# Expert blocks of 32 places instead of 64, with two buffers for the rows that come in and two for the results that go out

## The reference

```python
def hier_moe(xn, w_group, b_group, w_expert, b_expert, w1, w3, w2):
    """Top-1 expert group, then top-2 SwiGLU experts inside that group."""
    ...                                   # eid: 2 of 32 experts for each token, ew: their weights
    def expert_block(args):
        xb, e = args
        return (jax.nn.silu(xb @ w1[e]) * (xb @ w3[e])) @ w2[e]
    ...                                   # out[t] = sum over its two experts of ew * y
```

## Time and profile before

| | us |
|---|---|
| time of three runs | 1649.1, 1653.12, 1655.06 (median 1653.12) |
| the profiled execution's own time | 1650.04 |
| its span | 1648.4 |
| granted clock of TensorE over the span | 0.988 |
| PE busy | 1564.9 (95%) |
| DMA over the span | 328.42 MB, mean 199 GB/s |
| expert stage, first to last of its matmuls | 1050.4 to 1603.2 |

### The profile page before, as it was taken

The page is one execution under the profiler, slowest core; times in us unless marked ns, Lnnn a source line. Parts: engine busy times, 40 slices in busy tenths (PEclk is TensorE's granted clock), DMA queues, the critical chain, the costliest instruction groups (busy, mean ns, idle before and its releaser), DMA issues.

```text
span 1648.4 us, 21863 instructions
## 1 busy us (share of the span) xinstructions
PE 1564.9 (95%) x7698; PEld 848.1 (51%) x7699; DVE 560.9 (34%) x1542; ACT 346.8 (21%) x859; POOL 300.6 (18%) x431
## 2 busy tenths in 40 slices
PE   7999998999999999998999999799899999999986
PEld 4554544444444444444444555566466666666652
DVE  4210004766566656654222354511011111111115
ACT  3000002443343443433000111111111111111113
POOL 2000001322222222222001001221121212121114
PEclk9999999999999999998999999999999999999997
DMA  9214621553111110103443821699999989999928
GB/s 236 67 56 62 125 78 58 166 181 114 45 32 26 45 33 26 46 13 90 161 136 103 357 107 74 235 416 419 419 419 418 386 352 407 416 421 417 415 85 306
DMA packets 135914, 328.42 MB, mean 199 GB/s; under 512 B 40046, under 2 KB 80398, under 8 KB 126640
## 3 DMA queue, kind: packets, MB, share of 16 engines
q1 hardware_dynamic: 117472, 297.98, 49.5%
q0 software_dynamic: 9984, 17.62, 3.2%
q10 hardware_dynamic: 8400, 12.07, 2.1%
HBM read 276.09 MB, written 55.25 MB: 201 GB/s over the span
## 4 chain that ended last, share of the span: by engine, by line
PE 83%; DVE 7%; DMA 5%; issue 2%; ACT 2%; POOL 1%; SPq 1%; POOLq 0%; ACTq 0%; DVEq 0%
PE PS L856 17%; PE PS L707 12%; PE PS L591 11%; PE PS L870 9%; PE PS L745 7%; PE PS L780 7%; PE PS L693 4%; PE PS L654 4%; PE PS L673 4%; PE PS L586 3%; DMA WA<-w 2%; PE PS L833 2%; DMA BA<-hn_d,ids 1%; POOL WA L1532 1%; PE PS L573 1%
## 5 line engine op out<-in xcount | busy, mean ns | idle before, releaser
L707 PE MATMUL PS<-WA 128*128 128x512 f32 x512 | 255.0, 611 | 2.2 <-ACT WA L967 1.6
L856 PE MATMUL PS<-WA,BA 128*64 128x256 f32 x2048 | 227.6, 379 | 2.9 <-DMA WA<-w 1.5
L856 PEld LDWEIGHTS PS<-WA,BA 128*64 128x64 f32 x2048 | 173.9, 137 | 63.9 <-issue 17.3
L591 PE MATMUL PS<-WA,BA 128*128 128x512 f32 x416 | 180.1, 593 | 2.9 <-DVE WA L1090 2.9
L1450 POOL TENSOR_SCALAR BA<-BA,rin,gates 128x640 f32<-128x640 f32 (+7 forms) x128 | 99.6, 781 | 270.8 <-DVE rin L1209 270.8
L1364 DVE SCALAR_TENSOR_TENSOR BA<-BA,PS 128x256 f32<-128x256 f32 x46 | 19.4, 422 | 340.8 <-ACT BA L1029 340.8
L591 PEld LDWEIGHTS PS<-WA,BA 128*128 128x128 f32 x416 | 78.6, 190 | 99.6 <-issue 96.2
L673 PEld LDWEIGHTS PS<-ident,BA 128*128 128x128 f32 x648 | 79.4, 144 | 94.1 <-issue 86.6
L870 PE MATMUL PS<-WA,BA 128*64 128x512 f32 x512 | 116.9, 597 | 9.7 <-DVE BA L1374 8.7
L707 PEld LDWEIGHTS PS<-WA 128*128 128x128 f32 x512 | 84.6, 190 | 78.4 <-issue 67.6
L957 ACT ACTIVATE BA<-PS,ngm 128x640 f32<-128x640 f32 (+7 forms) x128 | 89.9, 702 | 130.5 <-DVE ngm L1187 126.1
(11 more groups left out here) (249 smaller groups left out, 1548.4 us busy)
## 6 DMA issues: line engine op xcount, KB each, us to landing
WA<-w SPq DMA_DIRECT2D x66, 2048.0 KB, 25.3
BA<-w SPq DMA_DIRECT2D x30, 2048.0 KB, 27.6
rows_d<-WA SPq DMA_DIRECT2D x8, 2048.0 KB, 9.5
rows_d<-BA ACTq DMA_DIRECT2D x92, 128.0 KB, 6.8
WA<-w_in SPq DMA_DIRECT2D x16, 512.0 KB, 5.6
gates_d<-WA SPq DMA_DIRECT2D x32, 256.0 KB, 2.4
WA<-gates_d SPq DMA_DIRECT2D x8, 1024.0 KB, 5.4
BA<-w_in SPq DMA_DIRECT2D x26, 256.0 KB, 6.1
```

The costliest lines, as they stand in the source:

```text
L591: mm = pe.matmul(PS[:, j % 4, :], ws[:, c % 6, k, :], hnT[:, k, 512 * h:512 * h + 512], start=(k == 0), stop=(k == KT - 1))
L707: mm = pe.matmul(PS[:, 6, :], gw[:, j, k, :], hnT[:, k, 512 * hf:512 * hf + 512], start=(k == 0), stop=(k == KT - 1))
L856: mm = pe.matmul(PS[DH * h:DH * h + DH, bank, 0:256], xT[:, k, :], w[par][:, k, 256 * h:256 * h + 256], start=(k == 0), stop=(k == KT - 1))
```

## The change

`SLOTS` becomes 32. An expert now has at least two blocks and otherwise as many as its places need; the total is made even. For the counts above 18 experts have two and 14 have three: 78 blocks.

- **Rows**: two buffers `rows_in` of 32 rows x 1024. POOL gathers into one while the other is used; DVE then spreads the 32 rows over 128 partitions (`spread_rows`, four copies of 32x256) into `xin`, and PE needs two transposes instead of four. The numbers of a block are one load of 32 entries, kept in one column for each buffer, so the copy of the numbers is gone; but before POOL loads numbers into a column it waits until the gather that read that column has landed (`x_blk` of the other side).
- **PE**: one block's W1 and W3 are 8 slices of four matmuls, each on a quarter of the array's columns (32). W2 is four steps of four matmuls of 256 columns. W2 of a block is no longer done behind its own hidden values but behind W1 and W3 of the next block (`put_out`); the next rows are transposed behind it (`next_rows`), then the hidden values once (`turn_hidden`).
- **ACT**: the result is copied in four copies of 32x256 into one of two buffers and stored with one DMA.
- **DVE**: the gate works on 64 partitions; `spread_rows` stands between the gate and the copy of the transposed hidden values.
- **Routing**: the rows of the first two blocks are fetched from one list of 64 numbers; the `mark` table and its 32 small matmuls go; DVE makes the number of blocks even (three small operations) and spreads block 1's rows.

```diff
-SLOTS = 64
-MAXB = NE + 2 * SEQ // SLOTS
+SLOTS = 32
+MAXB = 2 * NE + 2 * SEQ // SLOTS - 4
...
+            for k in range(KT):
+                for q in range(4):
+                    w = (W1, W3)[q // 2][par]
+                    mm = pe.matmul(PS[SLOTS * q:SLOTS * q + SLOTS, 0, 0:256], xT[:, k, :],
+                                   w[:, k, 256 * (q % 2):256 * (q % 2) + 256], start=(k == 0), stop=(k == KT - 1))
...
+        def put_out(n_done, par, landed):
+
+            pe.wait_ge(S["hT_done"], n_done)
+            pe.wait_ge(S["y_evac"], n_done)
+            pe.wait_ge(S[f"we{3 * par + 2}"], landed)
+            for j in range(2):
+                for h in range(2):
+                    for n in range(4):
...
+            with pe.Fori(lo + 1, hi) as b:
+                hidden_sums(b, par, landed)
+                put_out(b, par, landed)
+                next_rows(b)
+                turn_hidden(b)
...
+            for n in range(4):
+                y = nc.scalar.copy(ysb[side][:, 256 * n:256 * n + 256], PS[SLOTS * n:SLOTS * n + SLOTS, 3, 0:256])
+            y.then_inc(S["y_evac"], 1)
+            act.wait_ge(S["y_evac"], n_done + 1)
+            act.dma_start(rows_d[bass.ds(first, SLOTS), :], ysb[side]).then_inc(S[f"y_st{side}"], 16)
...
+        def spread_rows(side):
+
+            for q in range(4):
+                rows = dve.tensor_copy(xin[SLOTS * q:SLOTS * q + SLOTS, :], rows_in[side][:, 256 * q:256 * q + 256])
+            rows.then_inc(S["x_free"], 1)
...
+        with dve.Fori(0, total, 2) as b:
+            for side in range(2):
+                now = dve.snap(b + side)
+                hidden(now)
+                dve.wait_ge(S[f"x_blk{side}"], dve.snap(b * 8 + 32))
+                dve.wait_ge(S["x_tr"], dve.snap(b + side + 1))
+                spread_rows(side)
+                take_hidden(now)
...
-            pool.wait_ge(S["ids_in"], pool.snap(b * 32 - 32))
-            pool.wait_ge(S["x_tr"], pool.snap(b + 1))
-            pool.sem_inc(S["rows_due"], 1)
-            g.tensor_copy(ids[:, 1:2], ids[:, 0:1]).then_inc(S["ids_held"], 1)
...
+        with pool.Fori(2, total + 2, 2) as b:
+            for side in range(2):
+                pool.wait_ge(S["ids_in"], pool.snap(b * 16 + 16 * side - 16))
+                pool.wait_ge(S["x_free"], pool.snap(b + side - 1))
+                pool.sem_inc(S["rows_due"], 1)
+                g.indirect_dma_start(rows_in[side], None, hn_d[:, :], bass.IndirectOffsetOnAxis(ap=ids[0:SLOTS, side:side + 1], axis=0),
+                                     bounds_check=SEQ - 1, oob_is_err=False).then_inc(S[f"x_blk{side}"], 16)
+                pool.wait_ge(S[f"x_blk{1 - side}"], pool.snap(b * 8 + 16 * side))
+                load_ids(1 - side, pool.value_load(block_row_i[0:1, bass.ds(b + side + 1, 1)], min_val=0, max_val=NE * SEQ + FIRST))
```

More of the change, by code:

```diff
@@ L876, in _ @@
+        for e in range(NW):
+            expert(e, e, 16, None if e == 0 else 16)
+        with pe.Fori(1, NE // NW) as e3:
             for par in range(NW):
-                expert(e3 * NW + par, e3 + 1, par)
+                expert(e3 * NW + par, par, pe.snap(e3 * 16 + 16), pe.snap(e3 * 16 if par == 0 else e3 * 16 + 16))
         for e in range(NE - NE % NW, NE):
-            expert(e, e // NW + 1, e % NW)
+            expert(e, e % NW, 16 * (e // NW + 1), 16 * ((e - 1) // NW + 1))
+        total = pe.value_load(starts_i[0:1, NE:NE + 1], min_val=2 * NE, max_val=MAXB)
@@ new lines, in _ @@
+        gate_and_rows(0)
+        gate_and_rows(1)
+        put_rows(1, 0, 0)
+        with act.Fori(1, act.snap(total - 1), 2) as b:
+            for n in range(2):
+                gate_and_rows(act.snap(b + n + 1))
+                act.wait_ge(S[f"y_st{1 - n}"], act.snap(b * 8 + 8 + 16 * n))
+                put_rows(act.snap(b + n + 1), 1 - n, act.snap((b + n) * SLOTS))
+        act.wait_ge(S["y_st1"], act.snap(total * 8))
+        put_rows(total, 1, act.snap(total * SLOTS - SLOTS))
+        for n in range(2):
+            act.wait_ge(S[f"y_st{n}"], act.snap(total * 8 + 16))
@@ L1495, in _ @@
         scatter_ids(TT - 2)
-        pool.wait_ge(S["first_ids"], 1)
+        pool.wait_ge(S["first_ids"], 2)
         pool.wait_ge(S["hn_st"], 16 * TT)
-        g.indirect_dma_start(xin[:, :], None, hn_d[:, :], bass.IndirectOffsetOnAxis(ap=ids[:, 2:3], axis=0)) \
-            .then_inc(S["x_blk"], 16)
+        for n in range(2):
+            g.indirect_dma_start(rows_in[n], None, hn_d[:, :], bass.IndirectOffsetOnAxis(ap=ids[0:SLOTS, 2 + n:3 + n], axis=0)) \
+                .then_inc(S[f"x_blk{n}"], 16)
@@ L1500, in _, with load_ids @@
         scatter_ids(TT - 1)
-        pool.wait_ge(S["second_ids"], 1)
-        pool.wait_ge(S["x_tr"], 2)
-        g.indirect_dma_start(xin[:, :], None, hn_d[:, :], bass.IndirectOffsetOnAxis(ap=ids[:, 3:4], axis=0)) \
-            .then_inc(S["x_blk"], 16)
         pool.wait_ge(S["scattered"], 16 * 2 * TT)
-        def load_ids(row):
-            for n in range(2):
-                pool.dma_start(ids[SLOTS * n:SLOTS * n + SLOTS, 0:1], ids_d[bass.ds(row, SLOTS), n:n + 1],
-                               allow_slow_non_contiguous=True).then_inc(S["ids_in"], 16)
+        def load_ids(side, row):
+            pool.dma_start(ids[0:SLOTS, side:side + 1], ids_d[bass.ds(row, SLOTS), 0:1],
+                           allow_slow_non_contiguous=True).then_inc(S["ids_in"], 16)
```

220 lines of the change are left out of this document (96 added, 124 removed).

## The result

| kernel | median of the runs | lowest to highest | span of the profiled execution |
|---|---|---|---|
| before | 1653.82 us | 1649.1 to 1655.06 | 1648.4 us |
| changed | 1713.64 us | 1711.49 to 1717.49 | 1713.8 us |

The changed kernel takes 1.037 times as long as the one before, 95% interval 1.034 to 1.0399. That is some 61 us by the ratio, 59.8 by the medians. The forecast was 1704 us.

The account below looks back on a forecast made before the run. PE, busy 95% of the span, bounds the kernel before, with DMA also near its limit; afterwards POOL's chain would. 1650.0 + 53 (stage) - 1 (routing) = 1702 us by the profiled execution, predicted as 1704, range 1615 to 1755.

Parts of the forecast that it names:

- PE's block: PE's time per block without waits in the expert stage: sums 3.52, W2 1.73, uncovered rest 1.04, together 6.29 us.
- Rivals 3 and 4: Slower by PE: steps a quarter dearer, 1730 us, chance 0.09; quarters running pair after pair, about 2000 us, chance 0.02.
- rival 1: POOL's load of numbers takes only 4.8 to 5.3 us: 1603 us, up to 1612; chance 0.25.
- POOL's turn: POOL's serial turn per block: gather issue 1.07, load of numbers 7.0, start 0.2, together 8.3 us in loaded time.
- The decisive step: POOL's serial turn, one load of numbers in flight despite double buffers, sets the pace in loaded time; chance 0.54.
- L: Time of POOL's load of a block's numbers, taken as 7.0 us in loaded time, 2.1 us unloaded.
- The floor of the DMA engines: DMA engines must be busy for about 480 us of the expert stage, before and after, at 419 GB/s.
- The sum: Expert stage: 58 blocks in 480 us at 8.3 us, other 20 at 6.29, 126 us; 606 us against 552.7.

Follow-up runs that it names:

- e2: Changed kernel with an eighth of W1 and W3 and a quarter of W2 loaded from the fourth expert on: 1631.1 us.
- e6: Changed kernel with PE's block bounds loaded one expert ahead and nothing else: 1720.3 us, 1.0433 times before.
- e1: Changed kernel with the numbers of a block loaded two blocks ahead, two loads in flight: 1661.6 us, 1.0074 times before.
- e5: Changed kernel with numbers loaded two blocks ahead and PE's block bounds one expert ahead: 1660.1 us, 1.0059 times before.
- e4: Kernel before with the numbers of a block loaded two blocks ahead: 1649.15 us, 0.9996 times before.
- e12: Kernel of e5 gathering 128 quarter rows of 1 KB into 128 partitions instead of 32 whole rows into 32: 1631.7 us, 0.9902 times before.

## Why the prediction was right, point by point

- **PE's block.** Forecast 3.52 + 1.73 + 1.04 = 6.29 us, measured 6.22. The four quarters run together as the two halves did: 64 sums from 1300.23 to 1303.71, 3.48 us. Rivals 3 and 4 are out; the granted clock in the stretch from 1100 to 1250 us was 0.97. By an estimate from the Trainium skill's 2.38 times for three column tiles (TensorE: Matmul & The Clock Gate, section "Measured speedup vs the span model") the four would have cost a quarter more; the trace shows no such loss.
- **A term that was missing: the change of expert.** The prediction multiplied 6.29 by 78 and had nothing at the boundary of an expert, where PE's queue loads two bounds. It costs 0.9 us at a change, 1.56 at every third, 34 us in the stage of e2. To take it away gave no gain in the changed kernel (e6) and none behind e1 (e5), so POOL's chain and then the weights covered it. But it makes rival 1's 1603 to 1612 us too low: with hardly any weights to wait for, e2 still took 1631.1; e1, which is rival 1 made true (numbers hardly ever late), took 1661.6, and without the boundary stalls e5 still 1660.1.
- **POOL's turn.** Forecast 1.07 + 7.0 + 0.2 = 8.3 us, measured 8.74 in the loaded stretch. The load was a little quicker than taken (19 loads, mean 6.7), the issue 1.13 with the step to the load, but from landing to the next gather there are 0.88 us, not 0.2. I had dropped the 0.86 us that stood behind the copy in the earlier trace rows with the copy; but the gather starts as late behind the wait that is left (0.88). The errors are -0.3, +0.06 and +0.68 us, together +0.44, 5% of the turn. (My 7.0 left out two first loads of 2.3 and 2.4 us, issued at 1061.5 and 1317.6 us; the other 41 of the 43 issued from 1060 to 1572 us have a mean of 7.1.)
- **The decisive step held.** Only one load of numbers is in flight, two buffers or not; POOL waited for it in 58 turns, DVE for the gather, PE for DVE. Taking it away gave back 52 us (e1), and in the kernel before nothing (e4), as the prediction had said of the hidden chain. That L comes from running beside the weights is shown too: 2.0 us without them (e2).
- **The floor of the DMA engines was mis-sized.** 480 us stood on 419 GB/s. At the measured 391 to 395 the same 201 MB need some 510 us. This is the real fault of the prediction: it took the gather's new shape as if only its bytes counted. The forecast bore it, because POOL's chain stood above that floor (621.4 us of stage against 606). Rival 1 rested on the same 480 and on no term for the boundary, and would have missed by 50.
- **The sum with measured terms.** 510 / 8.74 = 58 blocks in loaded time and 20 x 6.22 = 124 more give 634; measured 621.4. The formula is a little too high, because the turn isn't 8.74 all through: from 1088 to 1575 us it was 8.16 in the mean, with stretches of a DMA share of 0.84 in it. So it is partly luck that the forecast came within 10 us: its terms were 28 us short of the measured ones, and the formula gives 13 us of that back. The mechanism is not luck; e1 and e4 test it alone.
- **The start and the end.** Not in the prediction: from 1060 to 1080 us PE was busy for 13.37 of 20 us at a granted clock of 0.83, waiting for the third block's rows (5.18 us at 1064.83). All kernels of the new form have it, e12 too (188 GB/s from 1050 to 1080, where the kernel before had 295). The kernel with hardly any weights has the wait as well (6.54 us at 1068.62). By the 3 MB that weren't moved in these 30 us it is worth some 8 us, an estimate at 417 GB/s; no run took it away.

What the 61 us are made of, counted by the ratios and from the fastest form back: blocks of 32 with rows gathered wide stand at 0.9902 (-16 us); the narrow gather takes that to 1.0059 (+26); the bounds at the boundary, nearly hidden behind it, to 1.0074 (+2); the single load of numbers in flight to 1.037 (+49). The sum is 61. The shares depend on this order: taken out of the changed kernel alone, the bounds gave nothing back (e6). And the -16 us stand for all else that the change did, not for the block's size alone.

## What to carry to other kernels

When blocks are made smaller, each chain per block that doesn't shrink with them comes to light: look for the one with a single load in flight, and price it at its latency beside the transfers that will run with it (here 6.6 us), not at that without them (2.0). And a gather is not only its bytes: 32 rows of 4 KB into 32 partitions took 26 GB/s from the total at a full DMA share, 128 pieces of 1 KB into 128 partitions nearly nothing (417 against 419 to 421). A small stall that an experiment removes without gain (the 0.9 to 1.56 us here) may still be real; its worth shows only once the limit above it is gone.

## What the runs showed of the hardware that I had not expected

- The weights' own rate at a full DMA share depends on the form of the transfers beside them: 0.585 MB per cent of 16 engines' time in 150 us beside narrow gathers, 0.622 to 0.626 beside wide ones or none. The share of 1.02 looked the same in both; only MB by share tells them apart.
- Gathering 128 pieces of 1 KB, their numbers computed on POOL (0.92 us for four instructions of 32 elements), cost less than gathering 32 pieces of 4 KB: 1631.7 us against 1660.1. The packets that the view counts were as many in both, some 80 for each gather and load of numbers.
- Halving PE's matmuls (82.3 instead of 124.9 busy us in 150) moved the transfers by 4 GB/s only (395 against 391), and by at most 1 in the two stretches behind: here PE's reads of the weights out of SBUF hardly touched the writing of the next ones.
- Two loads of a register from `starts_i` in PE's queue, with what goes with them, left PE idle for some 0.9 us more at a change of expert (e2), and for 1.56 where an outer loop turned as well.
